# Causal mask, minimum and normalisation of an attention stage moved between engines, and page numbers loaded ahead

## The chip, the cores and the metric

One NeuronCore of a Trainium2 chip runs the whole program. The metric is the device time of one execution in microseconds (us). The engines are PE (TensorE), DVE (VectorE), ACT (ScalarE), POOL (GpSimd) and SP (SyncE, which issues the DMAs). PEld is PE's weight loading.

## The reference

The program is one inference step of a two-layer decoder for a prompt of 1024 tokens and eight samples of four new tokens. Each layer projects its input, runs three groups of heads (an mLSTM, a causal pooling and a forgetting attention), projects their outputs, and ends in an MLP. The change touches the forgetting attention only: six heads of 64, on the prompt (block by block of 128 queries) and on the samples, which attend to 2048 cached keys in 16 pages each.

```
def fox_block(q, Fq, qpos, k, v, Ft, kpos):
    s = jnp.einsum("bqhd,bshd->bhqs", q, k) * (DH_C ** -0.5)
    s = s + jnp.swapaxes(Fq, 1, 2)[..., None] - Ft[:, :, None, :]
    s = jnp.where(qpos[:, None] >= kpos[None, :], s, -jnp.inf)
    p = jax.nn.softmax(s, axis=-1)
    return jnp.einsum("bhqs,bshd->bqhd", p, v)

def fox_sample(q, k, v, lf, cache_k, cache_v, cache_logf, page_table, l):
    kp = cache_k[l, page_table]
    vp = cache_v[l, page_table].reshape(B, P, H, dh).astype(jnp.float32)
    ...
    s_past = jnp.einsum("bqhd,bphd->bhqp", q, kp) * scale + Fq[..., None] - Ft[:, :, None, :P]
    ...
    p = jax.nn.softmax(jnp.concatenate([s_past, s_new], axis=-1), axis=-1)
```

F is the cumulated log-forget value. Everything is float32.

## The kernel before

Every layer has three stages: projection, attention, and output projection with MLP. Each is a block in which every engine has its own program, written out by hand; they meet only through semaphores. The order of each engine's work is therefore fixed.

The prompt's part of attention is cut into 24 units (`units`, L1432): three pairs of heads `j`, and for each pair eight blocks of 128 queries in the order 0, 7, 2, 5, 1, 6, 3, 4. A unit with block `qb` has (qb + 1) x 128 keys for each of its two heads `e`. The program's scores have their sign turned, so a softmax takes a minimum and an exponential of scale -1. For unit `i`:

- `query_key` (PE, L1581): products of queries and keys into PSUM banks 0 to 3. Two bf16 products of a one-hot matrix and `future` (L1594) then add the causal mask to the last 128 keys of each head.
- `lows` (DVE, L1746): one operation per head adds the keys' forget sums `Fb` to PSUM, writes `Trow` and leaves the minimum in `lowest`.
- `exps` (ACT, L1862): exponential in place, sum in `sums`. DVE inverts the sums (L1833).
- POOL multiplies `Trow` by the inverse (L1555), one operation per head.
- `turn` (PE, L1596): transposes of `Trow` in pieces of up to four blocks; `turned_copy` (L1720) copies them to `PT` on ACT or DVE, by the parity of piece and head.
- `mixed` (PE, L1606): values times `PT`; ACT copies the result to `F` (L1869).

PE's loop (L1695) does in step `i`: query_key of unit i, turn of i - 1, mix of i - 2. Between these stand the samples' steps, three steps of the loop for each of eight batches `b`: `scores` in step 3b, `past_turned` and the small transpose `new turned` in step 3b + 1, `past_mixed` in step 3b + 2. PSUM banks 4 to 7 are handed out in turn from one table (`slot_table`, L1446); a slot can be filled when the slot four places before it has been emptied (`has_room`, L1502).

The pages of cached keys and values (384 KB each, 128 for a layer) come through a ring of 24 buffers, six steps of four pages. SP loads a page's number from SBUF into a register (L1443) and issues the transfer (L1444). From the seventh step of four pages on it first waits until `past_mixed` has read the buffers of six steps ago (L1520). A batch uses four steps, so the buffers for the last two steps of batch b's scores are those that the first two steps of the mix of batch b - 1 free. Five pages (`early`, L1404) are issued at the end of the projection (L761). The samples' forget sums come by another transfer of 256 KB for a batch (`sums_of`, L1509).

After the last unit DVE subtracts for the first weight tile of the next stage (`wlo`, L1845) and copies the samples' output (`picked_out`, L1813).

## Time and profile before

| | us |
|---|---|
| median of 3 runs | 2901.68 |
| lowest, highest | 2898.79, 2908.41 |
| span of the profiled execution | 2905.2 |
| attention of layer 0 in it | 400.0 to 622.2 |
| attention of layer 1 in it | 1831.2 to 2047.4 |

| engine | busy us | share of the span |
|---|---|---|
| PE | 2763.6 | 95% |
| PEld | 2553.9 | 88% |
| DVE | 1186.2 | 41% |
| ACT | 659.8 | 23% |
| POOL | 424.7 | 15% |

The profiled execution's span is 3.5 us above the median and within the range of the runs. A timeline row has the start, the length, engine, line and operation, what is written and read, the shapes and the count of merged instructions; brackets hold the idle time of the engine before it and what ended it. The engines' busy time in a stretch stands with its count of instructions in parentheses. Matmuls of float32 appear as two records each. The granted clock is 1.00 at 2.4 GHz and 0.50 at 1.2 GHz. "SPq" is the queue of instructions of SP.

### The profile page before, as it was taken

The page shows a single profiled execution, that of the slowest core. Times are in us where ns is not written, and L with a number is a line of the kernel's source. Part 1 is how long each engine was busy: PE and PEld are TensorE (multiplying, and loading weights), DVE is VectorE, ACT ScalarE, POOL GpSimd, SP SyncE. Part 2 cuts the span into 40 slices and gives each one's busy share as a digit, 9 for nine tenths or more (in the row PEclk, how much of TensorE's full clock was granted, in tenths as well). Part 3 has the DMA queues.
Part 4 walks back from the last instruction along what each step waited for, and adds up shares of the span by engine and source line. Part 5 has one row for each costly group of instructions (what it writes and reads, how often), then busy time and mean ns, then how long its engine had stood idle before and what let it go on. Part 6 is the DMA issues. An engine that isn't in the chain of part 4 may idle for free. (4 is left out here: it accounts for less than half of the span.)

```text
span 2905.2 us, 48336 instructions
## 1 busy us (share of the span) xinstructions
PE 2763.6 (95%) x20492; PEld 2553.9 (88%) x20492; DVE 1186.2 (41%) x2069; ACT 659.8 (23%) x1122; POOL 424.7 (15%) x424
## 2 busy tenths in 40 slices
PE   5999988889999999999999999878999999999998
PEld 3999965569999999999989999545899999999998
DVE  5625524346532422424355344333564233242344
ACT  4334323333111111001133432333231001001011
POOL 1101114340000000001111000244300001001010
PEclk9999989899999999999999999899999999999999
DMA  7440157741222222111224101776302111111111
GB/s 299 146 105 30 64 193 272 252 148 44 66 88 84 81 84 73 59 44 44 66 106 117 48 30 66 267 262 223 125 31 86 54 49 44 44 59 44 44 58 68
DMA packets 106873, 295.36 MB, mean 102 GB/s; under 512 B 19606, under 2 KB 32791, under 8 KB 104611
## 3 DMA queue, kind: packets, MB, share of 16 engines
q1 hardware_dynamic: 106498, 291.49, 29.8%
q8 instruction: 162, 2.65, 0.4%
q0 software_dynamic: 160, 0.79, 0.1%
q14 instruction: 53, 0.43, 0.0%
HBM read 269.61 MB, written 22.63 MB: 101 GB/s over the span
## 5 line engine op out<-in xcount | busy, mean ns | idle before, releaser
L304 PE MATMUL PS<-hH,whi 128*128 128x352 f32 x1632 | 533.2, 327 | 8.0 <-DVE hL L2193 6.4
L304 PE MATMUL PS<-hL,whi 128*128 128x352 f32 x1632 | 523.8, 321 | 0.0
L304 PE MATMUL PS<-hH,wlo 128*128 128x352 f32 x1632 | 523.4, 321 | 0.0
L304 PE MATMUL PS<-aH,whi 128*128 128x352 f32 x1344 | 439.6, 327 | 9.2 <-DVE aL L251 9.1
L304 PE MATMUL PS<-aL,whi 128*128 128x352 f32 x1344 | 432.7, 322 | 0.0
L304 PE MATMUL PS<-aH,wlo 128*128 128x352 f32 x1344 | 432.4, 322 | 0.0
L292 POOL CAST whi<-raw 128x1024 fp32r<-128x1024 f32 x158 | 167.6, 1061 | 1672.6 <-PE PS L304 1336.5
L304 PEld LDWEIGHTS PS<-hH,whi 128*128 128x128 f32 x1632 | 306.7, 188 | 16.7 <-issue 11.8
L304 PEld LDWEIGHTS PS<-hL,whi 128*128 128x128 f32 x1632 | 307.4, 188 | 0.0
L304 PEld LDWEIGHTS PS<-hH,wlo 128*128 128x128 f32 x1632 | 306.4, 188 | 0.0
L824 PE MATMUL PS<-aH,whi 128*128 128x352 f32 x912 | 303.7, 333 | 1.9 <-ACT F L1022 1.9
L824 PE MATMUL PS<-aH,wlo 128*128 128x352 f32 x912 | 294.3, 323 | 0.0
L824 PE MATMUL PS<-aL,whi 128*128 128x352 f32 x912 | 294.0, 322 | 0.0
L304 PEld LDWEIGHTS PS<-aH,whi 128*128 128x128 f32 x1344 | 253.9, 189 | 14.1 <-issue 13.9
L297 DVE TENSOR_TENSOR wlo<-raw,whi 128x1024 fp32r<-128x1024 f32 x160 | 195.5, 1223 | 155.9 <-POOL whi L292 155.3
L304 PEld LDWEIGHTS PS<-aL,whi 128*128 128x128 f32 x1344 | 254.2, 189 | 0.0
L304 PEld LDWEIGHTS PS<-aH,wlo 128*128 128x128 f32 x1344 | 253.5, 189 | 0.0
L2162 ACT ACTIVATE ev<-PS 128x1056 f32<-128x1056 f32 x64 | 67.7, 1057 | 573.1 <-PE PS L304 573.1
L2277 DVE TENSOR_TENSOR aH<-ev 128x1056 fp32r<-128x1056 f32 x64 | 83.2, 1300 | 272.0 <-ACT ev L2162 272.0
L1555 POOL TENSOR_SCALAR Trow<-Trow,sums 128x128 f32<-128x128 f32 (+7 forms) x96 | 164.5, 1726 | 189.9 <-DVE sums L1833 189.9
L824 PEld LDWEIGHTS PS<-aH,whi 128*128 128x128 f32 x912 | 172.3, 189 | 8.5 <-issue 4.2
L824 PEld LDWEIGHTS PS<-aL,whi 128*128 128x128 f32 x912 | 172.7, 189 | 0.4
(353 smaller groups left out, 3840.8 us busy)
## 6 DMA issues: line engine op xcount, KB each, us to landing
KVp<-kv SPq DMA_DIRECT2D x256, 384.0 KB, 4.3
raw<-w_ff SPq DMA_DIRECT2D x128, 512.0 KB, 3.5
raw<-w_in SPq DMA_DIRECT2D x42, 512.0 KB, 3.5
wad_single<-w_ada SPq DMA_DIRECT2D x40, 512.0 KB, 3.5
wad<-w_ada SPq DMA_DIRECT2D x32, 512.0 KB, 5.5
x_spill<-x SPq DMA_DIRECT2D x2, 4224.0 KB, 13.9
wada<-w_first SPq DMA_DIRECT2D x8, 1024.0 KB, 7.2
raw<-w_out SPq DMA_DIRECT2D x16, 512.0 KB, 4.3
```

Of the source, the lines that this page charges most:

```text
L292: nc.gpsimd.tensor_copy(home(n)[0][:], raw[spot(n)][:]).then_inc(s["high"], 1)
L297: nc.vector.tensor_tensor(wl[:], raw[spot(n)][:], wh[:].bitcast(F32), ALU.subtract).then_inc(s["split"], 1)
L304: last = nc.tensor.matmul(PS[:, 3 * p + part, 0:CW], w[:, k, :], a[:, k, part * CW:(part + 1) * CW], start=k == 0 and w is wh and a is hig ...
L824: last = nc.tensor.matmul(PS[:, part, 0:CW], w[:, k, :], a[:, k, part * CW:(part + 1) * CW], start=k == 0 and w is whi[n % 2] and a is aH, ...
L1555: nc.gpsimd.tensor_scalar(Trow[i % 2][e][:, 0:n], Trow[i % 2][e][:, 0:n], sums[:, i % 4, e:e + 1], None, ALU.mult)\
L2162: nc.scalar.activation(three(ev[n % 2][:]), banks(n % 2), ACT.Relu).then_inc(s["room"], NCH)
L2277: link(nc.vector.tensor_tensor(aH[:, j, :], t, t, ALU.mult))
```

## The change

Causal mask: the two bf16 mask products on PE and their operands go. POOL adds the triangular mask to the 128 forget sums of the diagonal block for both heads of a unit (`mask_diagonal`), one unit ahead. DVE's minimum runs in two operations for a head, first the keys before the diagonal block, then the diagonal block with the first minimum as its start.

Normalisation: POOL's multiplication of `Trow` goes. The transposes wait for the exponential alone. DVE's reciprocal of the sums stays, later in DVE's order. PE spreads the inverse over the rows of the output by a product of the broadcast sums and the identity (`turn_inverse`), into the bank of the mix of the unit before; DVE copies it (`take_inverse`), and DVE, not ACT, moves the mix out of PSUM, with a multiplication.

Shared bank: the samples' small transpose goes into the same bank as the mix and the inverse, except for batch 0; DVE copies it. ACT's exponentials of the two heads stand before and behind its copies of the transposes.

Page numbers: SP loads several page numbers into registers first (seven at the start of attention, then eight, four, and 16 in one go for each four steps) ahead of the wait and issues the transfers from the registers. The early five are loaded together too.

```diff
-                for n in range(len(early)):
-                    page_in(sp, l, n)
+                for n, page in enumerate([page_number(sp, n) for n in range(len(early))]):
+                    page_in(sp, l, n, page)
...
+    diagonal = [tile(f"diagonal{i}", [P, 2, P], T0 + 1024 * i) for i in range(2)]
+    nearest = tile("nearest", [P, 4, 2], T0 + 2048)
+
+    norms = [tile(f"norms{i}", [P, P], T0 + 2112 + 512 * i) for i in range(2)]
...
+                def pages_of(i):
+                    return range(max(i * GP, len(early)), (i + 1) * GP)
+                numbers = {n: page_number(sp, n) for i in (1, 2) for n in pages_of(i)}
                 for b in range(3):
                     sums_of(b)
-                for i in range(NB * STEPS):
+                for i in range(1, NB * STEPS):
...
+                    if i >= 3 and (i - RING) % STEPS == 0:
+                        numbers = {n: page_number(sp, n) for m in range(i, min(i + STEPS, NB * STEPS)) for n in pages_of(m)}
+                    elif 3 <= i < RING and i % 2:
+                        numbers = {n: page_number(sp, n) for m in range(i, min(i + 2, RING)) for n in pages_of(m)}
                     if i >= RING:
                         sp.wait_ge(S["past_mixed"], i - RING + 1)
...
+                    for n in pages_of(i):
+                        page_in(sp, l, n, numbers[n])
...
+                def mask_diagonal(i):
+                    j, qb = units[i]
+                    for e in range(2):
+                        is_empty(pool, ("forget", j, e, qb // 4))
+                    if i >= 2:
+                        pool.wait_ge(S["low"], 2 * i - 2)
+                    tri = c("tri").rearrange("p (o n) -> p o n", o=1).to_broadcast([P, 2, P])
+                    nc.gpsimd.tensor_tensor(diagonal[i % 2][:], Fb[:, :, qb * P:(qb + 1) * P], tri, ALU.add).then_inc(S["diagonal"], 1)
+
+                mask_diagonal(0)
                 for i in range(NU):
-                    for e in range(2):
-                        n = (units[i][1] + 1) * P
-                        pool.wait_ge(S["shares"], i + 1)
-                        nc.gpsimd.tensor_scalar(Trow[i % 2][e][:, 0:n], Trow[i % 2][e][:, 0:n], sums[:, i % 4, e:e + 1], None, ALU.mult)\
-                            .then_inc(S["scaled"], 1)
+                    if i + 1 < NU:
+                        mask_diagonal(i + 1)
...
-                    for e in range(2):
-                        nc.tensor.matmul(PS[:, 2 * e + qb // 4, m - P:m], one_hot[:], future[:], start=False, stop=True).then_inc(S["qk"], 1)
...
-                        pe.wait_ge(S["scaled"], 2 * u + e + 1)
+                        pe.wait_ge(S["exp"], 2 * u + e + 1)
...
+                    if u + 1 < NU:
+                        turn_inverse(u + 1, bank[key])
+                    if (u + 2) % 3 == 1 and (u + 2) // 3 < NB:
+                        new_turned((u + 2) // 3, bank[key])
...
+                def turn_inverse(u, at_):
+                    pe.wait_ge(S["inverted"], u + 1)
+                    for e in range(2):
+                        nc.tensor.matmul(PS[hp(e), at_, P:2 * P], sums[:, u % 4, e:e + 1].to_broadcast([P, DH]), ident,
+                                         start=True, stop=True, skip_group_check=True)
+
+                def new_turned(b, at_):
                     pe.wait_ge(S["pad"], b + 1)
-                    nc.tensor.transpose(PS[0:NS, bank[key], 0:P], PN[:, b, :], ident).then_inc(S["filled"], 1)
+                    return nc.tensor.transpose(PS[0:NS, at_, 2 * P:3 * P], PN[:, b, :], ident)
...
+                        if e == 0:
+                            dve.wait_ge(S["diagonal"], i + 1)
+                        before, row = n - P, PS[:, 2 * e:2 * e + 2, :].rearrange("p a n -> p (a n)")
+                        if qb:
+                            link(nc.vector.tensor_tensor_reduce(out=Trow[i % 2][e][:, 0:before], in0=Fb[:, e, 0:before], in1=row[:, 0:before],
+                                                                scale=1.0, scalar=3.0e38, op0=ALU.add, op1=ALU.min,
+                                                                accum_out=nearest[:, i % 4, e:e + 1]))
+                        nc.vector.tensor_tensor_reduce(out=Trow[i % 2][e][:, before:n], in0=diagonal[i % 2][:, e, :], in1=row[:, before:n],
+                                                       scale=1.0, scalar=nearest[:, i % 4, e:e + 1] if qb else 3.0e38, op0=ALU.add, op1=ALU.min,
                                                        accum_out=lowest[:, i % 4, e:e + 1]).then_inc(S["low"], 1)
...
+                def mixed(u):
+                    j, qb = units[u]
+                    key = ("mixed", u)
+                    is_full(dve, key)
+                    b, part = divmod(u + 2, 3)
+                    if part == 1 and b < NB:
+                        new_turned(b, bank[key])
+                    if u + 1 < NU:
+                        link(take_inverse(u + 1, bank[key]))
+                    nc.vector.tensor_tensor(F[:, QC + j, qb * P:(qb + 1) * P], PS[:, bank[key], 0:P], norms[u % 2][:], ALU.mult).then_inc(S["dve"], 1)
...
+                    if i >= 2:
+                        mixed(i - 2)
                     if i < NU:
                         dve.wait_ge(S["exp"], 2 * i + 2)
-                        nc.vector.reciprocal(sums[:, i % 4, :], sums[:, i % 4, :]).then_inc(S["shares"], 1)
+                        invert(i)
...
-                        exps(i)
+                        exps(i, 0)
                     if 1 <= i <= NU:
                         turned_copy(act, copy, "act", i - 1)
+                    if i < NU:
+                        exps(i, 1)
...
-                    if i >= 2:
-                        mixed(i - 2)
```

## Rows read from the trace of the kernel before

**Rows 1.** Busy per engine, clock, DMA share, GB/s, of each layer's attention.
```profile
400.00:622.20 222.20, 183.94 (x2019) 114.16 (x2021) 81.91 (x213) 77.93 (x195) 90.25 (x81) 0.87 0.69 234
1831.20:2047.40 216.20, 177.90 (x2043) 113.58 (x2043) 81.47 (x213) 78.07 (x196) 90.32 (x81) 0.90 0.71 241
```

**Rows 2.** PE's waits in layer 0's attention: total us, times, longest.
```profile
PE PS L1603 <- POOL Trow L1555: 15.8, 14, 2.0
PE PS L1639 <- DMA KVp<-kv: 12.4, 7, 3.5
PE PS L1614 <- ACT PT L1850: 6.4, 3, 2.6
```

**Rows 3.** PE's waits in layer 1's attention.
```profile
PE PS L1603 <- POOL Trow L1555: 13.5, 12, 2.0
PE PS L1639 <- DMA KVp<-kv: 13.1, 7, 3.0
...
PE PS L1649 <- ACT PT L1850: 2.7, 3, 1.2
```

**Rows 4.** Timeline of PE, fourth batch: start, length, [idle before <- releaser].
```profile
500.68 2.79 PE L1663 MATMUL PS<-KVp,PTs 128*32 128x384 f32 x32
...
515.24 0.86 PE L1639 MATMUL PS<-KVp,Qb 128*32 128x128 f32 x24 [0.68 <-DMA KVp<-kv]
```

**Rows 5.** Timeline of SP, its issues.
```profile
502.31 8.41 SPq L1444 DMA_DIRECT2D KVp<-kv  x8
```

**Rows 6.** One line's instructions, L1443, layer 0: ns min/median/max.
```profile
L1443 SPq TENSOR_LOAD <-ptab x123: 262/269/298, 401.9 to 593.2; - x123
```

**Rows 7.** One line's instructions, L1444, layer 0.
```profile
L1444 SPq DMA_DIRECT2D KVp<-kv x123: 337/338/1766, 402.6 to 594.0; - x123
...
DMA to landing us min/median/max: 2.9/4.4/6.6
```

**Rows 8.** DMA queues from 434 to 448 us: packets, MB, share.
```profile
q1 hardware_dynamic: 1713, 4.68, 97.1%
```

**Rows 9.** Layer 0's eight half-clock stretches: one, and their sum.
```profile
567.20:574.00 6.80, 6.25 (x84) 5.33 (x88) 0.76 (x2) 0.87 (x2) 2.96 (x3) 0.50 0.95 318
...
sum 57.90, PE 52.54 PEld 32.44 DVE 11.77 ACT 13.23 POOL 13.48; mean PE 6.57 PEld 4.06 DVE 1.47 ACT 1.65 POOL 1.69
```

**Rows 10.** The sum of layer 1's seven.
```profile
sum 44.50, PE 38.82 PEld 28.79 DVE 7.51 ACT 9.31 POOL 17.55; mean PE 5.55 PEld 4.11 DVE 1.07 ACT 1.33 POOL 2.51
```

**Rows 11.** Timeline of PE, first batch.
```profile
433.86 1.09 PE L1603 MATMUL PS<-con,Trow 128*128 128x128 f32 x8 [0.65 <-POOL Trow L1555]
...
436.75 0.29 PE L1594 MATMUL PS<-future,one_hot 128*128 128x128 bf16 x2
436.87 0.50 PE L1603 MATMUL PS<-con,Trow 128*128 128x128 f32 x3
...
438.41 1.97 PE L1614 MATMUL PS<-PT,vC 128*64 128x128 f32 x32
```

**Rows 12.** Timeline of all engines from 515 to 526 us.
```profile
520.17 1.03 ACT L1866 ACTIVATE Trow<-Trow,lowest 128x896 f32<-128x896 f32 x1
...
521.61 1.75 PE L1614 MATMUL PS<-PT,vC 128*64 128x128 f32 x24 [2.60 <-ACT PT L1850]
```

**Rows 13.** Timeline of DVE from 583.9 us.
```profile
584.26 0.42 DVE L1755 CUSTOM_DVE_ANT_0 Trow<-Fb,PS 128x256 f32<-128x256 f32 x1 [4.54 <-PE PS L1594]
...
584.60 0.42 DVE L1755 CUSTOM_DVE_ANT_0 Trow<-Fb,PS 128x256 f32<-128x256 f32 x1
```

**Rows 14.** Groups by line and shape, POOL, layer 0's attention: busy, mean ns | idle.
```profile
L1555 POOL TENSOR_SCALAR Trow<-Trow,sums 128x256 f32<-128x256 f32 x6 | 5.5, 927 | 8.7 <-DVE sums L1833 8.7
```

**Rows 15.** Timeline of PE, start of layer 0's attention.
```profile
418.85 1.51 PE L1639 MATMUL PS<-KVp,Qb 128*32 128x128 f32 x24 [3.08 <-DMA KVp<-kv]
```

**Rows 16.** Timeline of SP, same stretch.
```profile
399.96 1.89 SPq L1511 DMA_DIRECT2D LFb<-past_sums  x3
```

**Rows 17.** Timeline of all engines, end of layer 0's attention.
```profile
620.70 1.23 DVE L1845 TENSOR_TENSOR wlo<-raw,whi 128x1024 fp32r<-128x1024 f32 x1 [0.21 <-DVE Sel L1809]
```

More of the change, by code:

```diff
@@ L1438, in trunk, with page_number, page_in @@
     slots = []
-    def page_in(sp, l, n):
+    def page_number(sp, n):
+        return sp.value_load(ptab[0:1, n:n + 1], min_val=0, max_val=kv.shape[1] - 1)
+    def page_in(sp, l, n, page):
         step = n // GP
-        page = sp.value_load(ptab[0:1, n:n + 1], min_val=0, max_val=kv.shape[1] - 1)
         sp.dma_start(KVp[n % (GP * RING)][:], kv[bass.ds(l, 1), bass.ds(page, 1)].rearrange("a c p n -> (a c p) n")).then_inc(sem(f"fox_kv{step % RING}"), 16)
@@ L1463, in slot_table @@
                 take(("past turned", b), "act")
-                take(("new turned", b), "act")
+                if i < 2:
+                    take(("new turned", b), "dve")
             if i >= 2:
-                take(("mixed", i - 2), "act")
+                take(("mixed", i - 2), "dve")
             if i == 0:
@@ L1666, in past_mixed @@
                         last.then_inc(S["past_mixed"], 1)
[L1667 removed]
+                    pe.wait_ge(S["new_out"], b + 1)
                     nc.tensor.matmul(PS[96:128, bank[key], 0:HC * DH], PTn[b % 2][:, 96:128], vC[0:NS, CH, :], start=False, stop=True,
@@ L1778, in scores, with invert, new_turned, take_inverse @@
                     nc.vector.tensor_tensor(low[:, b:b + 1], low[:, b:b + 1], low[:, NB + b:NB + b + 1], ALU.min).then_inc(S["min"], 1)
+                def invert(i):
+                    nc.vector.reciprocal(sums[:, i % 4, :], sums[:, i % 4, :]).then_inc(S["inverted"], 1)
+                def new_turned(b, at_):
+                    if b >= 2:
+                        is_full(dve, ("past mixed", b - 2))
+                    return nc.vector.tensor_copy(PTn[b % 2][:], PS[0:NS, at_, 2 * P:3 * P]).then_inc(S["new_out"], 1)
+                def take_inverse(u, at_):
+                    return nc.vector.tensor_copy(norms[u % 2][:], PS[:, at_, P:2 * P])
+                def mixed(u):
[8 more added lines that the diff above has]
+                    nc.vector.tensor_tensor(F[:, QC + j, qb * P:(qb + 1) * P], PS[:, bank[key], 0:P], norms[u % 2][:], ALU.mult).then_inc(S["dve"], 1)
                 def past_mixed(b):
@@ L1860, in forget, with exps @@
                         copy(Fb[:, 1, half * 512:(half + 1) * 512], PS[:, bank[key], :]).then_inc(S["act"], 1)
-                def exps(i):
+                def exps(i, e):
                     n = (units[i][1] + 1) * P
-                    for e in range(2):
-                        act.wait_ge(S["low"], 2 * i + e + 1)
-                        nc.scalar.activation(Trow[i % 2][e][:, 0:n], Trow[i % 2][e][:, 0:n], ACT.Exp, scale=-1.0,
-                                             bias=lowest[:, i % 4, e:e + 1], accum_out=sums[:, i % 4, e:e + 1]).then_inc(S["exp"], 1)
-                def mixed(u):
-                    j, qb = units[u]
-                    key = ("mixed", u)
-                    is_full(act, key)
-                    copy(F[:, QC + j, qb * P:(qb + 1) * P], PS[:, bank[key], 0:P]).then_inc(S["act"], 1)
+                    act.wait_ge(S["low"], 2 * i + e + 1)
+                    nc.scalar.activation(Trow[i % 2][e][:, 0:n], Trow[i % 2][e][:, 0:n], ACT.Exp, scale=-1.0,
+                                         bias=lowest[:, i % 4, e:e + 1], accum_out=sums[:, i % 4, e:e + 1]).then_inc(S["exp"], 1)
                 def past_exp(b):
@@ L1886, in past_turned @@
                     copy(PTs[b % 2][:], PS[:, bank[key], :].rearrange("p (k n) -> p k n", k=GP)).then_inc(S["act"], 1)
-                    key = ("new turned", b)
-                    is_full(act, key)
-                    copy(PTn[b % 2][:], PS[0:NS, bank[key], 0:P]).then_inc(S["act"], 1)
                 for i in range(NU + 2):
```

33 lines of the change are left out of this document (15 added, 18 removed).

## The prediction

> **What bounds it now.** The edits all lie in the attention stage, so I read the table of busy times by stretch first. Attention takes 222.2 us in layer 0 and 216.2 us in layer 1, 438.4 of 2905.2 us; PE is busy 83 and 82% of it, DVE, ACT and POOL about 40% each, and DMA 0.69 to 0.71 [rows 1]. A stretch is thus a PE stream with holes, and only a hole that closes is worth time. Then the waits of PE. Three kinds matter: the transposes of the probabilities wait for POOL's normalisation, 15.8 and 13.5 us; the past scores wait for key pages, 12.4 and 13.1 us; the mix waits for ACT's copies of the transposes, 6.4 us in layer 0 [rows 2, 3] and, by the like row, in layer 1. They add up to 67.6 us.
>
> The second kind is a loop that the change can tighten or run into. A page buffer is free when the mix of past values has read it, and the scores of the next batch, nine microseconds of PE work later, need pages loaded into the buffers freed by the first half of that mix: eight pages. In the fourth batch the mix starts at 500.68 and the last scores can start at 515.24, 14.56 us later [rows 4]. The other batches that wait show 14 to 16.6 us between the same two places. Those 14.56 us are: 0.9 until the first buffers are free and 0.7 until the first issue at 502.31; seven more issues, eight in 8.41 us, so (8.41 - 0.34) / 7 = 1.15 us apart [rows 5]; and about 4.4 us from an issue to its landing [rows 7]. An issue costs SP a register load of 0.27 us [rows 6], address steps and the DMA instruction itself, 0.34 us [rows 7]; from start to start it is 1.10 us, of which I read in SP's records 0.56 us for the page number and 0.54 for the rest. But the transfers are no quicker: q1 moved 4.68 MB in 14 us at a 97.1% share [rows 8], 334 GB/s, or 1.18 us for a page of 0.393 MB. Issue and transfer have nearly the same pace, so faster issue gains the start of a burst, not its rate.
>
> Last, the clock. PE runs at the lower of its two levels (1.2 of 2.4 GHz) in eight stretches of layer 0 and seven of layer 1, 57.9 and 44.5 us [rows 9, 10]; the one that opens each stage is 20.5 us. The 6.8 us from 567.20 follow two waits for POOL of 2.05 and 1.73 us. Without the two openings 61.4 us are left, with PE busy nearly throughout: half, some 29 us, is lost. Four of these stretches, 20.5 us, follow POOL waits.
>
> **The change part by part** (both layers; 48 units, a unit being a pair of heads with a block of queries).
>
> *Normalisation leaves POOL: -29.3.* The 96 multiplications go; PE's transposes wait for the exponential alone. All 26 waits for POOL go, like the 0.65 us at 433.86 [rows 11]: 15.8 + 13.5 [rows 2, 3]. What is late next is the exponential of the second head, which now stands behind ACT's copies of the unit before. Between the end of a unit's transposes and the second head's transposes of the next, PE has a mix, a query-key product and one head's transposes, at least 2.3 us; ACT has a copy (0.6) and an exponential (1.2 with its accumulator read, by the 1.03 us row [rows 12]). So it is covered, narrowly in the shortest units; bound 0 to +24 (0.5 us a unit), taken 0.
>
> *Exponentials split around the copies: -8.* At 521.61 the mix waited 2.60 us for a copy that stood behind both exponentials; the second began at 520.17 and cost 1.03 plus the read [rows 12]. The copy comes 1.2 us earlier, less 0.3 for the longer minimum: 0.9 for each of the six waits [rows 2, 3], -5.4; and some 2.6 from the 3.7 us that PE's transposes of the past waited for bank room behind the same copies (2.7 in layer 1 [rows 3], 1.0 in layer 0). Bounds 0 and -16.6.
>
> *Mask and inverse on PE: +5.4.* The two bf16 mask products take PE from 436.75 to 436.87, 0.12 us, up to 0.2 elsewhere [rows 11]; at 0.15 x 48 they give back 7.2. The inverse is two products of the shape of the mix, which does 16 in 1.9 us [rows 11]: 0.24 to 0.26, x 48 = 12.6 with waits for nothing, since the reciprocal follows the exponential that the transposes before it needed already.
>
> *DVE: 0.* Two operations for the minimum: the 256-column one starts 0.34 us after its twin [rows 13], one column costs 1 ns, so a second operation adds about 0.07 and its accumulator wait 0.1: 0.17 for a head, about what the missing mask product (0.2 in latency) gives. Multiplying, copying the inverse and the small copy add 0.6 to 0.8 us a unit, next to a query-key product of 0.5 to 1.8 us on PE. DVE rises from 82 to some 106 us in a stage; still half idle. Bounds -2 and +24 (the same half microsecond). The Trainium skill (VectorE: DVE Perf Modes, Rules for kernel authors) advises to minimise the count of VectorE operations; by it this split is a loss, and the trace agrees on the sign, at 0.17 us a head, off PE's path.
>
> *Diagonal sums on POOL: 0.* 256 columns; the nearest row is 0.93 us for a one-input operation of that size [rows 14], two inputs at most twice. It is made a unit ahead; behind POOL's waits for the past's exponential it still is a unit early. Where the keys' sums change (units 0, 8, 16) it adds about 1 us before DVE's minimum, next to 4.5 us or more of PE work.
>
> *Page numbers ahead: -10 in the loop, +4.4 at the start.* In the loop SP does 16 loads while it would wait, and then issues at 0.54 us. First issue 0.55 us earlier; the eighth page, seven transfers of 1.15 behind the first, lands at 0.95 + 3.2 + 8.05 = 12.2 us after the mix starts, not 14.5. PE needs 11.5 to 12.8 us to get there without POOL waits (11.6 and 12.0 in two batches that had none). Leftover waits 0 to 0.9 a batch, mean 0.5 for 14 batches: 7 in place of the 16.6 us that the loop's own waits make today (25.5 less 8.9 at the two openings). Bounds -16.6 and +14. At the start, seven loads of 0.56, 3.9 us, now stand ahead of the three sums' transfers that SP issued from 399.96 [rows 16] and of all pages; PE waited for the last of them until 418.85 [rows 15]. The queue was full there, and the tail lands 1.7 to 2.8 us later: 2.2 x 2. Bounds 0 and +7.8.
>
> *Tail: +1.2.* The 1.23 us subtraction for the next stage [rows 17] ran while PE mixed the last unit; now it stands on DVE behind that unit's multiplication, and the last copy follows it: 0.6 a layer.
>
> *Clock: -11.* Half of the 20.5 us after POOL waits is about 9.5 with PE busy 93%, and 1.5 from the rest. Bounds -2 and -20.
>
> Sum: -29.3 - 8 + 5.4 - 10 + 4.4 + 1.2 - 11 = -47.3 us. On the profiled 2905.2 us that is 2858; the median of the runs, 2901.7, is 3.5 us lower, and I take the sum off that: 2854.5.
>
> **Rivals.**
> 1. *The pages take it back.* If the eighth page still lands 14.5 us after the mix starts, PE's gains between the two places turn into waits for DMA. Of the 29.3 us, 22.6 lie between them, all but the waits in the tail and two at 494 to 497 us. What is left: 6.7 + 5.4 + 5 (batches with slack) + 4 clock - 1.5 - 4.4 - 1.2 = 14 us: 2888. For it: a full queue [rows 8]. Against: 0.55 us of load certainly leaves the path.
> 2. *VectorE and ScalarE order.* The reciprocal, the multiplication and the second exponential each now wait for PE inside DVE's and ACT's programs; half a microsecond for each of 48 units leaves 23 of the 47 us: 2878. The change would then not do what it says: transposes would wait for ACT instead of POOL. Against it stands that both engines are idle 60% [rows 1].
> 3. *Slower: SP becomes the bound.* If the DMA instruction is held until the queue has room, 16 pages go out at the transfer's 1.18 us, then 16 loads of 0.56 and the sums' issue: 18.9 + 9.0 + 1 = 28.9 us for a batch, against a mean of 25.3 now (three of 26 steps of 222.2 and 216.2 us [rows 1]). 14 x 3.6 = 50 us slower, 2952. It decides from the point where SP's round exceeds PE's new 22.2 us; at 0.34 us an issue [rows 7] it is 19. Against it, up to four pages were in flight without a stall; twelve would be new. The longest issue took 1.77 us [rows 7].
>
> The Trainium skill (DMA: Bandwidth & Descriptors, Latency and other measured facts) gives a register load from memory a floor of about 600 ns; by it, an estimate, the 16 loads take 14 us, SP is some 2 to 3 us late for each batch and the gain shrinks to about 10 us. The trace disagrees, at 0.27 us [rows 6].
>
> **Chances.** Forecast 0.58; pages 0.17 (2888); order 0.12 (2878); SP 0.08 (2952); something unseen and slower 0.05. The forecast's own range, from its terms' bounds mixed rather than all at an end, is 2830 to 2875. To leave out no more than two in ten the range takes in the first two rivals: 2830 to 2892. What can be told from no change is 0.3%, 8.7 us: faster holds the forecast and nearly all of both rivals, 0.80; same 0.09; slower 0.11.
>
> **What would show it.** Right: no wait of PE for POOL; stages of about 198 us; SP's loads done before the next release; PE's waits for pages under 10 us outside the openings; half-clock stretches under 45 us outside them. The openings' last page should land some 2 us later. Wrong: waits for DMA up by over 10 us (rival 1), waits of PE for ACT or DVE above 30 us (rival 2), DMA instructions on SP over 1 us (rival 3). What would break the sum most is the transfers' rate with more pages in flight, which no row shows.

## The result and the profile after

The changed kernel takes 2870.85 us (median of 4 runs, 2866.78 to 2873.5), the kernel before 2900.8 us beside it (4 runs, 2898.79 to 2908.41): a ratio of 0.9892, interval 0.9872 to 0.9913, or 30 us less. The forecast was 2854.5 us, 47.3 less, in a range of 2830 to 2892. The sign and the mechanism came out; a third of the gain did not.

| profiled execution, us | before | after | difference |
|---|---|---|---|
| span | 2905.2 | 2865.1 | -40.1 |
| up to the first attention | 400.0 | 398.0 | -2.0 |
| attention of layer 0, to the next stage's first product | 225.3 | 203.1 | -22.2 |
| between the two | 1205.9 | 1204.3 | -1.6 |
| attention of layer 1 | 218.4 | 203.3 | -15.1 |
| rest | 855.6 | 856.4 | +0.8 |
| in the two stages: PE idle | 81.0 | 49.7 | -31.3 |
| in the two stages: PE busy | 362.7 | 356.7 | -6.0 |
| in the two stages: PE at half its clock | 102.5 | 89.6 | -12.9 |

The stages end here at the first product of the next stage, 2 to 3 us later than in [rows 1]. A span is nearly 2 us shorter than the time of its run (2865.1 and 2866.78 us after). The profiled execution before was thus about 6 us above the median of its runs, the one after 4 below; so the profiles are 40 us apart and the medians 30.

The two stages after, in the columns of [rows 1]:

```profile
398.00:601.10 203.10, 178.75 (x2091) 112.49 (x2092) 105.60 (x356) 71.45 (x168) 26.06 (x58) 0.89 0.71 257
1805.40:2008.70 203.30, 177.97 (x2092) 111.66 (x2092) 105.85 (x356) 71.24 (x168) 25.99 (x58) 0.89 0.70 257
```

POOL fell from 90 to 26 us in a stage, DVE rose from 82 to 106, and DMA moved 257 instead of 234 GB/s. What PE waits for, after, layer 0 and then layer 1 (total us, times, longest), to be held against [rows 2] and [rows 3]:

```profile
PE PS L1658 <- DMA KVp<-kv: 14.3, 8, 4.2
PE PS L1679 <- ACT PT L1914: 2.4, 4, 1.1
PE PS L1668 <- ACT PT L1914: 1.7, 3, 0.7
PE PS L1693 <- ACT PTs L1914: 1.3, 2, 0.9
PE PS L1606 <- DVE lowest L1792: 1.1, 1, 1.1
```

```profile
PE PS L1658 <- DMA KVp<-kv: 15.3, 8, 3.9
...
PE PS L1606 <- DVE lowest L1792: 1.6, 1, 1.6
```

POOL is gone from the list. DMA, which had 12.4 and 13.1 us, has 14.3 and 15.3: the pages take more of PE's time than before, though their numbers are loaded ahead. Where these waits lie tells why. In the loop they fell from 16.6 to 11.3 us over the two layers; in the two openings they rose from 8.9 to 18.3.

**The loop.** The fourth batch after (the one of [rows 4, 5]), on PE's timeline and then on SP's:

```profile
498.32 2.14 PE L1693 MATMUL PS<-KVp,PTs 128*32 128x384 f32 x24
...
511.86 0.86 PE L1658 MATMUL PS<-KVp,Qb 128*32 128x128 f32 x24 [1.35 <-DMA KVp<-kv]
```

```profile
499.38 4.34 SPq L1448 DMA_DIRECT2D KVp<-kv  x8
```

The eight issues take 4.34 us where they took 8.41 [rows 5], and the first comes 1.06 us after the mix starts, not 1.63. Still the last scores start 13.54 us after the mix, against 14.56. The landings of three of the eight show where the lead went: the line's transfers issued at 499.38, 502.49 and 503.00 us (minimum, median and maximum are the same, since each stretch holds one):

```profile
DMA to landing us min/median/max: 3.2/3.2/3.2
```

```profile
DMA to landing us min/median/max: 7.0/7.0/7.0
```

```profile
DMA to landing us min/median/max: 8.8/8.8/8.8
```

The first lands as fast as ever; the eighth stands in the queue for 8.8 us, landing at 511.8. Read so for all 14 bursts, the medians are: first issue 1.64 us after the mix starts before, 1.07 after; last issue 9.59 and 5.36; last landing 14.59 and 13.17 (12.2 to 14.2). An issue 4.2 us earlier brings a landing 1.4 us earlier. The queue carries the rest.

**The opening.** SP and then PE at the start of layer 0's stage:

```profile
402.11 1.87 SPq L1516 DMA_DIRECT2D LFb<-past_sums  x3
404.18 11.67 SPq L1448 DMA_DIRECT2D KVp<-kv  x10
```

```profile
411.74 1.51 PE L1658 MATMUL PS<-KVp,Qb 128*32 128x128 f32 x24 [1.68 <-DMA KVp<-kv]
415.62 1.51 PE L1658 MATMUL PS<-KVp,Qb 128*32 128x128 f32 x24 [2.37 <-DMA KVp<-kv]
421.33 1.51 PE L1658 MATMUL PS<-KVp,Qb 128*32 128x128 f32 x24 [4.19 <-DMA KVp<-kv]
```

Before, the sums were issued at 399.96 [rows 16] and PE waited for its last page until 418.85 [rows 15]. Both are 2 us or more later, in a stage that started 2.0 us earlier: 23.3 instead of 18.9 us from the start of the stage to the last scores of the first batch.

**The clock.** The longest stretch at half speed opens each stage, in both kernels. In the columns of [rows 9], the two stretches after:

```profile
400.20:427.50 27.30, 19.05 (x181) 11.91 (x180) 4.12 (x13) 4.17 (x9) 3.61 (x11) 0.50 0.83 299
1809.90:1833.80 23.90, 13.80 (x166) 9.33 (x163) 2.20 (x11) 3.06 (x8) 2.37 (x6) 0.50 0.91 318
```

Together they are 51.2 us with PE busy for 32.9. Before, the same two are 41.0 us long, PE busy for 32.1:

```profile
403.30:423.80 20.50, 15.69 (x175) 10.55 (x174) 2.15 (x11) 3.58 (x8) 2.05 (x7) 0.50 0.98 341
1833.50:1854.00 20.50, 16.38 (x176) 11.04 (x176) 2.77 (x12) 3.90 (x9) 2.73 (x11) 0.50 0.96 322
```

So the longer stretches hold more waiting, not more work at half speed.

### The profile page after: what moved, and what is told of

Same layout as the page of the kernel before. It is cut to its first block and busy times, and to the rows that moved or that the text cites. A ratio compares the mean times of both kernels' runs of the same rounds, so it can differ in the third digit from the quotient of the medians.

```text
span 2865.1 us, 48746 instructions
## 1 busy us (share of the span) xinstructions
PE 2754.0 (96%) x20588; PEld 2547.6 (89%) x20588; DVE 1232.8 (43%) x2349; ACT 643.3 (22%) x1058; POOL 291.5 (10%) x372
## 5 line engine op out<-in xcount | busy, mean ns | idle before, releaser
L304 PEld LDWEIGHTS PS<-hH,whi 128*128 128x128 f32 x1632 | 307.4, 188 | 16.1 <-issue 12.7
L304 PEld LDWEIGHTS PS<-aH,whi 128*128 128x128 f32 x1344 | 253.2, 188 | 14.4 <-issue 14.2
L304 PEld LDWEIGHTS PS<-aH,wlo 128*128 128x128 f32 x1344 | 253.0, 188 | 0.0
L824 PEld LDWEIGHTS PS<-aH,wlo 128*128 128x128 f32 x912 | 172.5, 189 | 0.0
```

What stands on the lines that cost most here:

```text
L304: last = nc.tensor.matmul(PS[:, 3 * p + part, 0:CW], w[:, k, :], a[:, k, part * CW:(part + 1) * CW], start=k == 0 and w is wh and a is hig ...
L824: last = nc.tensor.matmul(PS[:, part, 0:CW], w[:, k, :], a[:, k, part * CW:(part + 1) * CW], start=k == 0 and w is whi[n % 2] and a is aH, ...
```

## The experiments

Each ratio is to the kernel before, run beside it on the same chip. Not all were run on one chip, and the medians of the kernel before are 2900.1 to 2903.3 us, so between experiments the ratios are the better measure. The first theory was that of the forecast: PE's stream and the page loop are two limits that lie close together, and the change moves both. The rivals were that one part carries the gain alone, and that the pages take it back.

**Page numbers one by one again.** In the changed kernel, the numbers are no longer loaded ahead:

```diff
-                numbers = {n: page_number(sp, n) for i in (1, 2) for n in pages_of(i)}
...
                     for n in pages_of(i):
-                        page_in(sp, l, n, numbers[n])
+                        page_in(sp, l, n, page_number(sp, n))
```

> The changed kernel with the page numbers loaded one by one again, each in front of its transfer, at the end of the projection and all through attention; the rest of the change stays. Theory A (the numbers ahead pay in the loop and cost at the opening): from the start of a past mix to the last scores step it takes 14.5 us again in every batch, so PE waits for pages outside the openings rise from 11.3 us (both layers) to 30-36; the openings' waits fall from 18.3 to about 9 us and their half-clock stretches from 51 to about 41 us. Net 8 to 16 us slower than the changed kernel's 2871: 2879 to 2887. Theory B (the numbers ahead gain nothing in the loop, the transfers' pace sets it): only the opening changes, 2857 to 2862.

Measured: 2889.25 us, 0.9961 (0.9949 to 0.9973). The last page of a burst lands 14.39 us after the mix starts (median of 14), as before the change, and the loop's waits for pages are 31.9 us in the two layers. The time is 2 us above theory A's range. Of the change's 30 us, 19 hang on the numbers, and the rest, without them, is worth 11.

**Page numbers ahead, alone, in the kernel before.**

```diff
+                numbers = {n: page_number(sp, n) for i in (1, 2) for n in pages_of(i)}
...
-                        page_in(sp, l, n)
+                        page_in(sp, l, n, numbers[n])
```

> The kernel before with the page numbers loaded ahead and nothing else changed. Theory A: the openings cost 9 us more wait and some 4 us of clock; in the loop the waits for pages fall from 16.6 to 3-6 us, because PE, still held by POOL, reaches the last scores 13 to 14 us after the past mix and the pages are there after 12 to 13. Net within 4 us of before: 2897 to 2905. Theory B: only the opening's cost is left, 2910 to 2915.

Measured: 2898.02 us, 0.9994 (0.9978 to 1.0009): nothing that can be told from no change, as theory A had it. PE's waits in layer 0:

```profile
PE PS L1612 <- POOL Trow L1564: 17.5, 15, 2.1
PE PS L1648 <- DMA KVp<-kv: 7.7, 4, 4.1
```

The loop's waits for pages fell from 16.6 to 1.3 us in the two layers, but those for POOL rose from 15.8 to 17.5 and from 13.5 to 16.6, and the openings' from 8.9 to 15.8. The last page lands 12.75 us after the mix starts, and PE, held up by POOL, comes no sooner.

**Late normalisation, alone.** The changed kernel with the mask on PE and the numbers one by one: only the reciprocals, the shared bank and the order on ACT are left of the change.

```diff
+                        nc.tensor.matmul(PS[:, 2 * e + qb // 4, m - P:m], one_hot[:], future[:], start=False, stop=True).then_inc(S["qk"], 1)
...
-                        page_in(sp, l, n, numbers[n])
+                        page_in(sp, l, n, page_number(sp, n))
```

> Late reciprocals, the shared bank and ACT's order alone, on the kernel before: mask on PE with one minimum, page numbers one by one. Theory A: the 29.3 us of waits for POOL and some 8 us for ACT's copies go, but the last scores still come 15 us after the past mix starts and waits for pages grow from 16.6 us to over 32 in the loops: only 6 to 12 us below before, 2889 to 2895, and 2 to 6 us above the kernel without numbers ahead (2889.3). Rival: the pages do not bind and 25 us or more are gained, 2875 or below.

Measured: 2898.11 us, 0.9985 (0.9972 to 0.9997). The waits for POOL are gone, 29.3 us of them, and some 4 us of time with them. Layer 0's longest waits:

```profile
PE PS L1645 <- DMA KVp<-kv: 20.6, 8, 3.8
PE PS L304 <- DVE hL L2228: 2.7, 1, 2.7
```

With layer 1's 24.7 that is 45.3 us for pages, against 25.5 before: 19.8 us more, where 29.3 us of waits for POOL went, and the last page lands 14.93 us after the mix starts. The time missed theory A's range, 2889 to 2895, by 3 us. This is rival 1 of the prediction, in the kernel in which the pages were not sped up. Alone, the two main parts give 0.06 and 0.15%; with both, mask on PE (below), it is 1.31%. With the mask on GpSimd it is the same: numbers alone 0.06%, all the rest alone 0.39%, the whole change 1.08%. They don't add up, they unlock each other.

**Half of every page.** In both kernels only the keys' half of a page is transferred, and the mix of the past reads keys in place of values: the same instructions, half the bytes.

```diff
-        sp.dma_start(KVp[n % (GP * RING)][:], kv[bass.ds(l, 1), bass.ds(page, 1)].rearrange("a c p n -> (a c p) n")).\
+        sp.dma_start(KVp[n % (GP * RING)][:, 0:HC * DH], kv[bass.ds(l, 1), bass.ds(page, 1), :, 0:HC * DH].rearrange("a c p n -> (a c p) n")).\
...
-                                                    KVp[GP * (i % RING) + q][:, HC * DH:2 * HC * DH], start=step == 0,
+                                                    KVp[GP * (i % RING) + q][:, 0:HC * DH], start=step == 0,
```

> The kernel before with half of every page left out: only the 1536 bytes of keys in each row are transferred, and the past mix reads the keys in the values' place, so transfers of pages are 24 MB a layer in place of 48 and PE, DVE, ACT and POOL do what they did. Theory A (pages are the second bound of the stage): the loop's waits for pages (16.6 us) and most of the openings' (8.9 us) go, and with them some half-clock stretches, 5 to 10 us: 2866 to 2874. Rival: PE waits for POOL or ACT where it waited for pages, and under 10 us come back: above 2890.

> The changed kernel with the same half of every page left out. Theory A (what the change fell short by went into pages): loop waits 11.3 and openings' 18.3 us go, with 5 to 10 us of clock: 2830 to 2838, so 36 to 42 us below the kernel before with half pages, where the whole pages gave 30. Rival E (the shortfall is on DVE, ACT or in PE's added products): the difference of the two half-page kernels stays 28 to 32 us, 2838 to 2845.

Measured: 2884.09 us, 0.9936 (0.9918 to 0.9954), for the kernel before with half pages; 2847.91 us, 0.9811 (0.9793 to 0.983), for the changed one. Half the bytes are worth 19 us before the change and 22 to 24 after it. From the first issue of a burst to its last landing (differences of the medians of 14 bursts) it takes:

| us | one issue every 1.1 us | one every 0.5 to 0.6 us |
|---|---|---|
| whole pages | 12.95 | 12.1 |
| half pages | 10.7 | 8.7 |

So whole pages are held by their bytes once the issue is quick, and the old pace of issue alone takes 10.7 us. Layer 0 of the changed kernel with half pages:

```profile
PE PS L1658 <- DMA KVp<-kv: 6.6, 3, 4.9
PE PS L1679 <- ACT PT L1914: 2.4, 4, 1.1
```

These 6.6 us all lie in the opening. In the loop no wait for pages is left; the last one lands 9.8 us after the mix starts. So the 11.3 us of the loop are a matter of bytes, and no order of issue takes them all away. The opening is one of issue: even at half the bytes it takes 21.4 us, more than the 20.4 of the kernel before. Here not only the seven loads at its head count. PE's first batch needs pages up to the fourth step, and SP loads the next eight numbers ahead of that step's four pages: in layer 0 the seventh page goes out at 410.49 and the next at 415.87, and the transfers run dry between them (in the columns of [rows 1], a share of 0.29):

```profile
413.00:416.50 3.50, 2.67 (x48) 1.64 (x40) 0.00 (x0) 0.00 (x0) 0.00 (x0) 0.50 0.29 102
```

The absolute times were forecast 10 us too low in both kernels. In the kernel before, waits for POOL grew from 29.3 to 34.2 us and 5.4 of the openings' 8.9 stayed; in the changed one 12.8 of the openings' 18.3 us, which theory A let go, stayed. Their difference, 36.2 us, is near the low end of what theory A gave. With the pages out of the loop the change is worth 36 us, 4 to 6 more than with them.

**The opening's pages one by one.** The changed kernel, with the numbers ahead only from the first wait on.

```diff
-                numbers = {n: page_number(sp, n) for i in (1, 2) for n in pages_of(i)}
...
-                        page_in(sp, l, n, numbers[n])
+                        page_in(sp, l, n, numbers[n] if i >= RING else page_number(sp, n))
```

> The changed kernel with the opening's pages (up to the sixth step) loaded and issued one by one, after the three sums, as before; the numbers ahead stay in the loop and for the early five pages. Theory A: the openings' waits for pages fall from 18.3 to 9 us and the half-clock stretches there from 51 to 41 us: 2871 - 9 - 4 = 2858, between 2855 and 2862. Theory C (the opening costs what the prediction said, 4.4 us, and the rest of the shortfall lies in the loop): 2865 to 2868.

Measured: 2869.65 us, 0.9891 (0.987 to 0.9912), the changed kernel's time, above the ranges of both theories. The openings shrank as theory A had it, from 24.8 and 25.1 us to 19.7 and 21.5, and the waits moved one batch on:

```profile
PE PS L1655 <- DMA KVp<-kv: 5.0, 2, 3.0
```

That is layer 0 from 424 to 470 us. SP now does the opening's loads between the transfers and reaches the 16 loads of the first loop batch late: its first issue comes 4.2 us after the mix starts in layer 0 and 3.7 in layer 1, where 1.7 is usual. What a load costs is not gone when it is moved off one wait; it has to end where SP waits anyway.

**The opening's numbers in the projection.** The changed kernel, with the seven numbers loaded behind the early pages, at the end of the projection.

```diff
+                for n in range(len(early), 3 * GP):
+                    ahead[n] = page_number(sp, n)
...
-                numbers = {n: page_number(sp, n) for i in (1, 2) for n in pages_of(i)}
+                numbers = dict(ahead)
```

> The changed kernel with the seven page numbers of the opening loaded at the end of the projection, where SP waits anyway, so that the sums and seven pages are issued at once at the start of attention. Theory A: the last page of the opening lands 2 to 3 us earlier than in the kernel before, the openings' waits for pages are 3 to 7 us for both layers in place of 18.3, and the half clock there shrinks with them: 2848 to 2856. Theory C: 2862 to 2866. If the transfers and not the issue set the opening, it equals open_single.

Measured: 2862.91 us, 0.9876 (0.9857 to 0.9896), 5 to 8 us better than the changed kernel (by the ratios and by the medians), which the intervals don't part. The openings take 23.5 and 20.1 us, and PE's waits in them 8.7 and 6.2 us, where theory A wanted 3 to 7 for both together. Why layer 0's opening stayed long in this execution, although its first sums were issued at its very start, is open.

**Mask back on PE.** The changed kernel with two bf16 products for the mask and one minimum.

```diff
-                dve.wait_ge(S["diagonal"], i + 1)
...
+                        nc.tensor.matmul(PS[:, 2 * e + qb // 4, m - P:m], one_hot[:], future[:], start=False, stop=True).then_inc(S["qk"], 1)
```

> The changed kernel with its mask part undone: the two bf16 mask products on PE, one operation of DVE for a minimum, nothing on POOL; late reciprocals, shared bank and page numbers ahead stay. Theory A (PE's order and the pages bound the stage): 48 times 0.15 us more on PE, of which the waits for pages hide up to half: 3 to 8 us slower than the changed kernel's 2870.9, 2874 to 2879. Rival F (the second DVE operation and the diagonal sums are on the path): 2 to 6 us faster, 2865 to 2869.

Measured: 2867.01 us, 0.9869 (0.9847 to 0.989): 4 us below the changed kernel by the medians and 7 by the ratios, not above it, as the rival had it. The mask on GpSimd was to save PE 7.2 us, and by the trace it does save about 7.6: the two products take 0.12 us in front of transposes (30 times, [rows 11]) and 0.22 in front of other work (18 times). They end in waits. A second pair points the same way: the combined kernel below has 0.984 with the mask on PE against 0.9876 with it on GpSimd. With the numbers one by one the comparison goes the other way: 0.9961 with the mask on GpSimd against 0.9985 with it on PE. Every step is about the size of the intervals, which touch or overlap, so no gain or loss of this part is shown, within some 10 us either way; whether it turns with the page loop is open.

**ACT's exponentials together.** The changed kernel, both exponentials of a unit ahead of ACT's copies.

```diff
                         exps(i, 0)
+                        exps(i, 1)
...
-                    if i < NU:
-                        exps(i, 1)
```

> The changed kernel, but ScalarE makes both exponentials of a unit ahead of its copies of the unit before, as the kernel before does; all else of the change stays. Theory A (the prediction's term: the copy that stands behind both exponentials comes 1.2 us late, in the units whose mix needs it at once): 5 to 10 us slower than the changed kernel's 2871, so 2876 to 2881, with PE's waits for ScalarE's copies 6 us or more above the changed kernel's 10. Rival B: PE's transposes now wait for the exponential alone, and the second exponential comes 0.3 to 0.6 us earlier when it stands ahead of the copies, so that the order is a wash: 2868 to 2873. Rival C: copies come later, but the time goes into waits that pages set anyway: ScalarE's waits up by 5 us, DMA's down by as much, 2868 to 2873.

Measured: 2874.85 us, 0.9898 (0.9879 to 0.9918); 4 us over the changed kernel by the medians, under 2 by the ratios, neither A's 5 to 10 nor clearly B's nothing. The mechanism shows in layer 0's waits:

```profile
PE PS L1679 <- ACT PT L1914: 4.6, 4, 1.6
PE PS L1668 <- ACT PT L1914: 3.9, 3, 1.6
PE PS L1693 <- ACT PTs L1914: 1.2, 2, 0.6
```

ACT's waits rise from 10.0 to 19.4 us in the two layers, as much as the order was said to save and a bit more, and the time by less than half of it.

**The changed kernel once more.**

> The changed kernel itself, once more, for the spread of its time and of its profile. The prediction was set against one profiled execution of the kernel before, whose span of 2905.2 us lay at the high end of its runs, while that of the changed kernel, 2865.1, lay at the low end. Theory A (the executions of one kernel differ by some 10 us in when the pages land, and the change is worth the 30 us of the medians): 2866 to 2874, with a profile whose waits for DMA in the attention stages differ by up to 5 us from the first, and stages of 203 to 208 us. Rival B (the profiles' difference of 40 us is the change's own): 2858 to 2864.

Measured: 2870.28 us, 0.9893 (0.9876 to 0.9909), profile span 2866.6, stages of 202.0 and 202.9 us, waits for DMA of 17.4 and 16.1 us where the first profile has 14.3 and 15.3. So the change is worth 30 to 32 us; the other 8 to 10 of the profiles' 40 are one execution against another. Single profiles differ by 1 to 3 us in a stage's waits for pages.

**Combined.** Opening numbers in the projection, mask on PE.

> The changed kernel with two things altered: the seven page numbers of the opening are loaded at the end of the projection, where SyncE has time, and the causal mask goes back to two small products on PE, with one VectorE operation for the minimum. The two alone gave 2862.9 and 2867.0 against 2871. Theory A (they add up, the first by 8 and the second by 4 us): 2857 to 2861. Rival B (the second is worth nothing and lay within the spread of the runs): 2861 to 2866. Rival C (pages bound the loop, so that an earlier PE only waits more for them): 2863 to 2870, with the loop's waits for DMA above 14 us in the two layers.

Measured: 2856.92 us, 0.984 (0.9821 to 0.9859), at the good end of theory A; against the changed kernel the intervals are apart. Layer 0:

```profile
PE PS L1652 <- DMA KVp<-kv: 9.9, 8, 3.1
PE PS L1673 <- ACT PT L1902: 1.9, 3, 1.1
PE PS L1662 <- ACT PT L1902: 1.2, 2, 0.7
```

With layer 1's 8.4, pages cost 18.3 us instead of 29.6; 4.8 and 3.5 of it lie in openings of 20.4 us each, 10.0 in the loop.

**All opening numbers in the projection.** The combined kernel, with the numbers up to the sixth step loaded there too. These are 19 in all (seven, eight and four), not the 15 that the expectation speaks of.

```diff
-                for n in range(len(early), 3 * GP):
+                for n in range(len(early), RING * GP):
```

> The combined kernel (mask on PE, opening numbers loaded in the projection), but with all 15 page numbers of the opening loaded there: the seven that PE needs first and the eight of the next steps, so that SyncE issues 15 pages in the attention stage without a load between them, and reaches the loads of the first loop batch 4.5 us earlier. Theory A (SyncE's loads still cost the first loop batches something): the waits for pages of the first two loop batches, 2 us a layer in the combined kernel, go, 2853 to 2856. Rival B (the transfers are the limit once the issue is early: 15 pages at 1.02 us each land no sooner, and the eight that are not needed yet share the queue with the seven that are): the opening's waits, 4.8 and 3.5 us, stay or rise by up to 2 us, 2857 to 2862. Rival C: the eight loads hold back the store of the values at the end of the projection by 1.3 us, and nothing else changes: 2855 to 2858.

Measured: 2854.88 us, 0.9841 (0.9825 to 0.9858): the combined kernel's ratio. The waits of the first two loop batches fell (1.84 to 0.20 us in layer 0), the opening's rose to 5.6 and 5.4, and the loop kept 10.4 us in all. So the eight loads in the middle of the opening don't hold whole pages back: without them the last page that PE waits for is issued in layer 0 9.3 us after the first sums and not 13.2, and lands no sooner, 19.7 and not 18.9 us after them. Rival B's mechanism, A's number; the two can't be told apart in time.

## Why the prediction was right, and where a third of it went

By its own terms, in the two stages of the profile pair (us):

| term | predicted | measured | from |
|---|---|---|---|
| waits for POOL | -29.3 | -29.3 | none left, [rows 2, 3] |
| ACT's copies and the order | -8 | -8.3 | 18.3 to 10.0 |
| waits for DVE | 0 | +1.3 | minimum and copies |
| pages in the loop | -10 | -5.3 | 16.6 to 11.3 |
| opening | +4.4 | +9.4 | 8.9 to 18.3 |
| tail | +1.2 | +0.9 | 2.25 to 2.69 a layer |
| PE's added less removed work | +5.4 | about +7 | below |
| clock | -11 | about -11 | below |
| not traced | | -2 | |
| sum | -47.3 | -37.3 by the profiles | 443.7 to 406.4 |

**Normalisation, ACT, tail, DVE: right.** The second exponential behind the copies did not become the next wait (rival 2): the inverse's product waits for ACT 2.4 us in a layer, and DVE, at 106 us a stage as forecast, costs PE 2.7 us of waits for its minimum where it cost 3.3, and 1.9 us for its copies where it cost none. POOL's diagonal sums never came late. They take 0.73 us each in layer 0, less than the 0.93 of the one-input row [rows 14], so the bound of twice that was far off:

```profile
L1568 POOL TENSOR_TENSOR diagonal<-Fb,con 128x256 f32<-128x256 f32 x24 | 17.4, 729 | 59.1 <-DVE lowest L1792 26.8 <-ACT Fb L1914 18.0 <-DVE Fb L1774 7.4
```

The tail grew as described; before and after, the last products of the stage and the first of the next:

```profile
622.00 1.05 PE L1691 MATMUL PS<-Sel,OsB 128*64 128x12 f32 x32
625.30 0.63 PE L304 MATMUL PS<-hH,whi 128*128 128x352 f32 x1 [2.25 <-DVE hL L2193]
```

```profile
597.36 1.06 PE L1721 MATMUL PS<-Sel,OsB 128*64 128x12 f32 x32
601.10 0.40 PE L304 MATMUL PS<-hH,whi 128*128 128x352 f32 x1 [2.69 <-DVE hL L2247]
```

**Pages in the loop: the term that was mis-sized.** The working had the first landing 3.2 us behind its issue and each further page 1.15 us behind the one before, 12.2 us after the mix starts. It measured 13.17. The first landing was right. (The other batches that wait have 13.5 to 16.6 us between mix and last scores, not 14 to 16.6.) But from the first issue to the eighth landing is 12.1 us, not 11.25, so seven pages take 1.27 us each behind the first. The 1.15 was SP's old issue pace; the queue's own, 1.18 by its 334 GB/s [rows 8], was the better of the two and still short. Before the change the same stretch was 12.95 us: issue and transfer, read as having nearly the same pace, were held mainly by the bytes, and the slow issue added only a microsecond. The half pages show the two apart: 10.7 us by the old issue, 8.7 by the new. The queue is full when it matters:

```profile
502.00:512.00 10.00, 8.22 (x152) 6.87 (x154) 5.15 (x19) 3.25 (x9) 0.00 (x0) 1.00 0.99 343
```

That is the fourth batch again, in the columns of [rows 1]: a DMA share of 0.99 at 343 GB/s. The last page of a burst is held longest. In that batch the seventh lands at 509.45 (502.49 + 7.0) and the eighth 2.4 us later (503.00 + 8.8), while most land 1.0 apart. The Trainium skill (DMA: Bandwidth & Descriptors, Why a DMA increments its semaphore by 16 and not by 1) says that an intermediate count doesn't tell which bytes have landed, since with several transfers on one semaphore the later ones' completions fill the count of the earlier. Four pages share a semaphore here, and the trace agrees as far as it can show it: in the medians of the 14 bursts the eighth is 1.8 us behind the seventh and the fifth only 0.8 us behind the fourth, and in the burst of the mix that starts at 452.63 it is even recorded 0.6 us before the fourth. Then the 1.0 us between the fifth, sixth and seventh is no page's own time, and the group's end is the only landing to reckon with.

**Opening: the loads ahead were seen, what hides them was not; the size is off by a factor of two.** "Seven loads of 0.56, 3.9 us" ahead of everything was right: SP's sums start at 402.11, 4.1 us into the stage. That a full queue would leave only 2.2 us of it was the step that failed. PE's wait grew by 9.4 us in the two layers, 4.7 each, and the opening by 4.4 us each (20.4 and 20.7 to 24.8 and 25.1): all of the loads' time arrives. The queue that [rows 8] shows full is that of the loop. At the start it runs dry while SP loads; after, in the columns of [rows 1]:

```profile
398.00:402.00 4.00, 3.98 (x8) 1.68 (x8) 0.40 (x1) 0.41 (x1) 2.95 (x13) 0.77 0.16 67
402.00:404.20 2.20, 2.20 (x14) 0.99 (x12) 1.29 (x5) 1.29 (x3) 1.10 (x2) 0.50 0.17 59
```

Before, the same 4 us, and the next five, were

```profile
400.00:404.00 4.00, 4.00 (x10) 1.55 (x12) 1.38 (x2) 0.66 (x2) 3.39 (x15) 0.91 0.56 186
404.00:409.00 5.00, 5.00 (x61) 4.36 (x62) 0.67 (x5) 2.69 (x6) 1.20 (x2) 0.50 1.01 343
```

So the loads stand ahead of an idle queue. From the issue of the first sums to the landing of the last page that PE waits for it is 18.9 and 19.2 us before the change, 19.2 and 19.1 after it; only the start of this stretch moved, by 4.1 us in layer 0 and 4.5 in layer 1. The prediction also left out that eight more loads stand ahead of the last four of these pages; with whole pages the queue has the first seven to carry meanwhile, and they cost little (the last experiment). Both the waits, +9.4, and the openings' length, +8.8, are beyond even the bound of +7.8. Moving the loads to the projection, where SP waits anyway, won 5 to 8 us, within the intervals, and 10 by the medians with the mask on PE (2867.01 to 2856.92), which supports this; moving them behind the transfers won nothing, since the first loop batch then pays.

**PE's work and the clock.** From its start to the next group's, without waits, the inverse takes 0.27 us for a unit and 0.37 where the samples' transpose follows, 14.7 us in all and not 12.6; the mask products that went were about 7.6, near the 7.2 forecast. So +7 for +5.4. PE's busy time at half its clock outside the openings fell from 59.3 us (91.4 in [rows 9, 10], less 32.1) to 36.6 (69.5 by the same view, less 32.9); half of the 22.7 us is 11.3, the term as forecast. How near is partly luck: in the second profile of the changed kernel the same reckoning gives 30.6 us and a term of 14, since the stages are 82 us at half speed there and not 90. Busy time as a whole fell by 6.0 us, where 7 - 11.3 gives 4; the last 2 us are not traced.

**The rivals.** Rival 3, SP as the bound, did not come: 16 loads take 8.8 us and delay the first issue in only one of the 14 bursts, by 0.2 us; they end 0.04 us before the mix starts in the fourth batch, so the room is small. In that batch no issue of the eight took over 0.72 us, though by the eighth six other pages were under way. There is a trace of it: over both layers 37 of 256 issues took over 0.5 us and nine over 1 us, where it was nine and two before; up to ten pages were in flight, not four. SP's rows for the loads and for the transfers in layer 0, after:

```profile
L1443 SPq TENSOR_LOAD <-ptab x123: 261/267/541, 398.0 to 559.2; - x123
```

```profile
L1448 SPq DMA_DIRECT2D KVp<-kv x123: 332/333/1817, 404.2 to 569.3; - x123
```

The medians, 267 and 333 ns, and the longest issue, 1.8 us, are those of [rows 6, 7]. Rival 1 came in a small part: the waits for pages rose by 4.1 us over the two layers (25.5 to 29.6), and all of that in the openings. For the late normalisation alone it is the larger part: 19.8 of 29.3 us.

**What stays open.** The medians differ by 30 us, the two stages of the profiles by 37. The prediction took its terms from one profile, which stood above the median of its runs, and 7 of those 37 us lie within what one execution differs from another; which term they belong to can't be told. The table's terms therefore fit the pair of profiles and not the medians, of which they explain 7 us too much. Whether the mask belongs on PE or GpSimd is open within 10 us, and why the eighth page lands late was not tried.

## What to carry to other kernels

Before costing a removed wait, look for the loop that runs beside it and ask how much slack that loop has; here the page numbers alone were worth 0.06%, which is no difference that can be told, the late normalisation 0.15% (0.39% with the mask moved), and both together 1.1 to 1.3%. When instructions of a queue are moved ahead, they must end in time in which that queue waits anyway, the start of the stage included: seven loads at the head of a stage cost all of their 4 us, and with the same loads one stage earlier the program was 5 to 10 us faster. An issue pace near the transfer pace hides the latter, and even the pace by the queue's bytes, 1.18 us a page, was short of the 1.27 that was measured; a run with half the bytes tells which of the two binds.

## What the runs showed of the hardware

- Eight issues of 384 KB pages in 4.34 us met hardly a stall (seven steps of 0.52 us would be 4.0 with the last issue), and the last page was 8.8 us on its way behind the others. In all of layer 0 the longest way of a page was 12.3 us, and 6.6 before [rows 7].
- From the first issue to the eighth landing is 12.95 us at an issue every 1.1 us and 12.1 at one every 0.5 to 0.6: nearly twice the issue rate, 7% more transfer. With half the bytes it is 10.7 and 8.7.
- GpSimd's sum of two 128 x 256 f32 inputs takes 0.73 us, less than its 0.93 for a one-input multiplication by a scalar per partition of that size [rows 14].
